# Sixteen modulation sums of the first mix moved from VectorE to GpSimd products with ScalarE sums

## The chip, the cores and the metric

One NeuronCore of a Trainium2 chip runs the whole program in one launch. The metric is the device time in microseconds (us). TensorE (PE) does the matrix products, VectorE (DVE) and ScalarE (ACT) the elementwise work, GpSimd (POOL) little, and the queue of SyncE (SP) issues nearly all the DMAs. Everything is float32; a weight tile is split into a high part (`ring_hi`) and a low part (`ring_lo`), and each product is made of three matmuls.

## The reference, cut to what matters

The first of two stacked networks has two layers. In each, a vector `c` gives 48 columns of modulation, which shift, scale and gate the mixer and the feed-forward part:

```python
c_act = jax.nn.silu(c)
for l in range(DEPTH):                       # DEPTH = 2
    mod = (c_act @ w_ada[l] + b_ada[l])[:, None, :]          # 6 * 1024 numbers
    shift1, scale1, gate1, shift2, scale2, gate2 = jnp.split(mod, 6, axis=-1)
    h = rms_norm(x, norm1_g[l]) * (1.0 + scale1) + shift1
    z = h @ w_in[l]                          # 14 column tiles of 128
    ...                                      # windowed attention, short convolution, pooling
    x = x + gate1 * (mix @ w_out[l])         # 8 column tiles
    h2 = rms_norm(x, norm2_g[l]) * (1.0 + scale2) + shift2
    x = x + gate2 * peer_ffn(h2, ...)
```

x has 256 tokens of 1024 features and lies with the features on the partitions. Modulation column k (of 48) is a dot product of `c_act` with 1024 weights for each of 128 partitions, so one column costs one 128x1024 weight unit (512 KB), one product with `CROW` (silu of c, the same row on all partitions) and one sum along the row.

## The kernel before

The program is a sequence of blocks; at the end of each all engines meet. The blocks that matter here are the mix of layer 0 and the mix of layer 1, which come from one loop over `layer` (the block that starts at L651), and the block behind each (L1175), which begins with a norm that needs modulation columns 24 to 39.

Weights come as units of 128x1024 into a ring of 8 slots (`stream`, L255: the load of unit n waits until unit n-7 has been used). ScalarE copies a unit to `ring_hi` (`split_high`, L351), VectorE subtracts it to `ring_lo` (`split_low`, L358, its instruction at L361), TensorE multiplies (24 matmuls for a unit, L309 to L311). The mix block has 14 input units; their results are drained by ScalarE (L866 to L871) and go into rotations (L983 to L987, VectorE), scores with their maxima (`take_score`, L994 and L996), exponentials on ScalarE (L884), probabilities (L1015), pooling (L1073 to L1080), convolution (L1085 to L1099) and the low parts of the mixed operand (`attended_low`, L1021). Then 8 output units follow; a first group of three units shares its passes (its last instruction is at L838), and VectorE adds each result, times the gate, to the residual (L1120, "x_mixed"). A norm over x ends the block: squares on ScalarE (L421), sums on TensorE (L427), the root (L435), its inverse on VectorE (L440).

Each engine's order is written out by hand. Each waits in that order, so whatever stands at the head of a queue holds back all behind it. In layer 0 alone 24 more modulation columns (`N_LATE`) are worked out inside the mix: the queue of SP loads their units into three buffers (`late_units`, L657, DMA at L662; the load of unit k waits for the sum of unit k-3), and VectorE does product and sum in one instruction (`modulation`, L967, instruction at L971, which is followed by the read of its accumulator). Their places in VectorE's order: 4 behind the split of unit 3, 2 behind the second rotation, 3 behind the second pair of scores (L1055), 3 ahead of the first "x_mixed" (L1114), and 12 between the "x_mixed" of the output units. SP's order is: late units 0 to 5, the rest of the input units, late 6 to 8, output units 0 to 3, late 9 to 11, output units 4 to 7, and then the first 8 units of the next block (`S_WQ`) with late units 12 to 23 between them. GpSimd does three memsets in this block (L678 to L680) and nothing else. In layer 1 there are no late units.

Of the kernel before, what the change touches and what calls it, by code (L numbers as in the profile page):

```python
# [33 lines left out]
D = 1024  # L34
# [118 lines left out]
def program(nc, wstream, consts, mixconst, crow, xT, memT, pos, vec2, s5b, s5c, wglu, wdt, out):  # L153
    ctx = ExitStack()
    with ctx:
# [45 lines left out]
        def S(name):  # L201

            if name not in named:
                named[name] = pools[0][len(named)]
            return named[name]
# [49 lines left out]
        def stream(sp, u0, u1):  # L255

            for n in range(u0, u1):
                sp.wait_ge(units_used, n - (SLOTS - 1))
                sp.dma_start(RING[:, n % SLOTS, :], wstream[STREAM[n]]).then_inc(loaded[n % SLOTS], 16)
# [91 lines left out]
        def split_high(act, u, fresh):  # L351

            arrived(act.eng, u)
            if not fresh:
                act.eng.wait_ge(units_used, u - HIGHS + 1)
            act.mark(act.eng.activation(RING_HI[:, u % HIGHS, :], RING[:, u % SLOTS, :], ACT.Copy), "high")  # L356
# [268 lines left out]
        for layer in range(DEPTH):  # L625
# [19 lines left out]
            PU, P2, P4, P8, P16 = (a(2, T + 16) for _ in range(5))  # L645
            PL = a(2, T)
            MIX, MIX_LO, MIX_HI = a.split(8, T)
            ADB = [late[:, i, :] for i in range(3)]
            N_LATE = N_ADB - HOISTED if layer == 0 else 0
            VALUES, POOLED, CONV_X, CONV_C, CONV_B = 5, 6, 8, 10, 12  # L650
            with nc.Block() as block:  # L651
                @block.sync
                def _(sp):
                    sp.dma_start(AR[:, D:2 * D], mixconst).then_inc(S("mix_consts"), 16)
                    sp.dma_start(PK[:, :], wstream[layer * PER_LAYER + U_PARAMS + 1][:, 0:512]).then_inc(S("pool_keys"), 16)

                    def late_units(k0, k1):  # L657

                        for k in range(k0, min(k1, N_LATE)):
                            if k >= 3:  # L660
                                sp.wait_ge(S("modulated"), k - 2)
                            sp.dma_start(ADB[k % 3], wstream[layer * PER_LAYER + U_ADB + k])\  # L662
                                .then_inc(S(f"late{k % 3}"), 16)

                    late_units(0, 6)
                    stream(sp, S_IN + SLOTS, S_OUT)
                    late_units(6, 9)
                    stream(sp, S_OUT, S_OUT + 4)
                    late_units(9, 12)
                    stream(sp, S_OUT + 4, S_OUT + 8)  # L670
                    for i in range(N_OUT):
                        stream(sp, S_WQ + i, S_WQ + i + 1)
                        late_units(12 + 3 * i // 2, 12 + 3 * (i + 1) // 2)

                @block.gpsimd
                def _(pool):

                    pool.memset(VP, 0.0).then_inc(S("cleared"), 1)  # L678
                    pool.memset(CU, 0.0).then_inc(S("cleared"), 1)
                    pool.memset(PU, 0.0).then_inc(S("cleared"), 1)  # L680

                @block.tensor
                def _(pe):
# [168 lines left out]
                def _(sc):  # L852
# [3 lines left out]
                    def next_high(i):  # L856

                        split_high(act, S_IN + i, False)

                    def drain(i):  # L860

                        sc.wait_ge(units_used, used(S_IN + i))
                        src = PS[:, 2 + i % 3, 0:T]
                        if i < VALUES:
                            gain = L_KG if i == 0 else L_QG
                            act.mark(sc.activation(QSQ[:, i, :], src, ACT.Square), "qk_squares")  # L866
                            act.mark(sc.activation(Z[:, i, :], src, ACT.Copy, scale=LV[:, gain:gain + 1]), "z_copied")
                        elif i in (POOLED, POOLED + 1):
                            act.mark(sc.activation(PU[:, i - POOLED, 8:8 + T], src, ACT.Copy), "z_copied")
                        else:  # L870
                            act.mark(sc.activation(Z[:, i, :], src, ACT.Copy), "z_copied")  # L871

                    def head_std(n, bank, o, name):

                        act.wait("head_sums", n)
                        act.mark(sc.activation(QS[:, o], PS[:, bank, o], ACT.Sqrt, bias=EPS_COL, scale=1.0 / 64), name)

                    def exponentials(j):

                        act.wait("maxes", 2 * j + 2)  # L880
                        o = slice(4 * j, 4 * j + 4)
                        act.mark(sc.activation(ESK[:, o], ESK[:, o], ACT.Exp), "sink_exp")
                        for i in range(4 * j, 4 * j + 4):
                            act.mark(sc.activation(SC[:, i, :], SC[:, i, :], ACT.Exp, bias=NMX[:, i:i + 1],  # L884
                                                   scale=QI[:, i:i + 1], accum_out=SUM[:, i:i + 1]), "exps")
# [7 lines left out]
                    def attended_high(j):  # L893

                        act.wait("attended", j + 1)
                        act.mark(sc.activation(MIX_HI[:, j, :], PS[:, j % 2, 0:T], ACT.Copy), "mix_high")

                    split_high(act, S_IN + PRE, True)
                    act.wait("cleared", 3)
                    drain(0)  # L900
# [3 lines left out]
                    drain(2)  # L904
                    head_std(1, 5, slice(16, 20), "key_std")
                    next_high(6)
                    drain(3)
                    next_high(7)
                    drain(4)
                    next_high(8)  # L910
                    head_std(5, 1, slice(0, 16), "q_std")
                    drain(5)
                    next_high(9)
                    drain(6)
                    next_high(10)
                    act.wait("v_turned", 1)
                    vt = PS[:, 5, 0:T].rearrange("p (k h d) -> p k h d", k=2, h=2)
                    act.mark(sc.activation(VP[:, :, 0, 0:64], vt[:, :, 0, :], ACT.Copy), "v_padded")
# [1 line left out]
                    drain(7)  # L920
                    exponentials(0)
                    next_high(11)
                    drain(8)
                    next_high(12)
                    exponentials(1)
                    drain(9)
                    next_high(13)
                    exponentials(2)
                    probs_copy(0)
                    probs_copy(1)  # L930
                    drain(10)
                    split_high(act, S_OUT, False)
                    exponentials(3)
                    act.mark(sc.activation(RT[:, 0:1], EPS_COL, ACT.Sqrt), "root_table")
                    attended_high(0)
# [1 line left out]
                    probs_copy(3)  # L937
                    drain(11)
                    split_high(act, S_OUT + 1, False)
                    attended_high(1)  # L940
                    probs_copy(4)
                    probs_copy(5)
                    split_high(act, S_OUT + 2, False)
                    attended_high(2)
                    probs_copy(6)
                    probs_copy(7)
# [6 lines left out]
                        act.mark(sc.activation(MIX_HI[:, 4 + i, :], MIX[:, 4 + i, :], ACT.Copy), "conv_high")  # L953
                    attended_high(3)
                    split_high(act, S_OUT + 3, False)
                    for i in range(N_OUT):
                        if i + HIGHS < N_OUT + PRE:
                            split_high(act, S_OUT + i + HIGHS, False)
                        square_chunk(act, i, "x_mixed")
# [4 lines left out]
                def _(dve):  # L964
# [87 lines left out]
                    take_score(2)  # L1052
                    take_score(3)
                    maxes(1)
                    modulation(6, 9)  # L1055
                    low(11)
                    take_score(4)
                    take_score(5)
# [52 lines left out]
                                                 ALU.subtract), "conv_low")  # L1111
                    attended_low(3)
                    split_low(v, S_OUT + 3, N_IN + 3 - PRE)
                    modulation(9, 12)  # L1114
                    if layer == 0:
                        v.wait("modulated", 8)
                        v(dve.tensor_tensor(MOD[:, 16:24], MOD[:, 16:24], LV[:, L_BADA + 16:L_BADA + 24], ALU.add), "mod")
                    for i in range(N_OUT):
                        dve.wait_ge(units_used, used(S_OUT + i))
                        v.mark(dve.scalar_tensor_tensor(X[:, i, :], PS[:, 2 + i % 3, 0:T], col(MOD[:, 16:24], i),  # L1120
                                                        X[:, i, :], ALU.mult, ALU.add), "x_mixed")
                        if i + HIGHS < N_OUT + PRE:
                            split_low(v, S_OUT + i + HIGHS, N_IN + i + HIGHS - PRE)
                        modulation(12 + 3 * i // 2, 12 + 3 * (i + 1) // 2)
                    if layer == 0:
                        v.wait("modulated", N_LATE)
                        v(dve.tensor_tensor(MOD[:, 24:40], MOD[:, 24:40], LV[:, L_BADA + 24:L_BADA + 40], ALU.add), "mod")
                        v(dve.tensor_scalar(S1G[:, 8:16], MOD[:, 32:40], 1.0, None, ALU.add), "mod")
                        v(dve.tensor_tensor(S1G[:, 8:16], S1G[:, 8:16], LV[:, L_N2:L_N2 + 8], ALU.mult), "mod")
# [1775 lines left out]
```

## Time and profile before

| | us |
|---|---|
| median of 3 runs | 2463.84 |
| lowest, highest | 2461.8, 2473.33 |
| the profiled execution | 2463.14 |
| its span, first to last instruction | 2461.3 |

| engine | busy us | share of the span | instructions |
|---|---|---|---|
| PE matmul | 2364.9 | 96% | 14280 |
| PE weight load | 2123.6 | 86% | 14280 |
| DVE | 1797.1 | 73% | 2913 |
| ACT | 1157.5 | 47% | 1707 |
| POOL | 148.3 | 6% | 141 |

Busy time is a share of the whole span; the two mix blocks are two short stretches of it, of about 115 and 100 us. In the timeline a row is: start, duration, engine, line, operation, output<-input, shape, count, and in brackets how long the engine sat idle before it and what ended the wait. Starts are us from the span's start. A row with a count above 1 merges instructions that follow each other without a gap. Consecutive VectorE instructions overlap a little in the records: a 128x1024 operation that shows 1.22 us is followed by the next one 1.13 to 1.15 us after its start.

### The profile page before, as it was taken

To read this page: it belongs to the slowest core of one execution; us is meant where nothing else is said; L and a number is where in the kernel's file an instruction comes from. 1 tells how busy PE (TensorE), PEld (TensorE's weight loads), DVE (VectorE), ACT (ScalarE), POOL (GpSimd) and SP (SyncE) were. 2 spreads that over 40 slices of the span, in tenths; PEclk is the share of its full clock that TensorE was granted. 3 is DMA by queue.
4 is the path that set the end of the run, shared out by engine and by line. 5 is a ranking of instruction groups with operands and counts; after the bars stand their busy time and mean duration, and the time that the engine had idled before them with its cause. 6 is when DMAs were issued, how large, how long until landed. Compare 5 with 4: busy or idle time off the path is not lost. (4 is left out here: it accounts for less than half of the span.)

```text
span 2461.3 us, 36638 instructions
## 1 busy us (share of the span) xinstructions
PE 2364.9 (96%) x14280; PEld 2123.6 (86%) x14280; DVE 1797.1 (73%) x2913; ACT 1157.5 (47%) x1707; POOL 148.3 (6%) x141
## 2 busy tenths in 40 slices
PE   4979999999999999999999999999999999999998
PEld 4879898888888888889899888888888888898998
DVE  7979997677667676678999676566767576555665
ACT  4542255444545454564135444455545523544554
POOL 0000153000000000000045100000000000000000
PEclk9989999999999999999999999999999999999999
DMA  9365544787676666434544586665555523343553
GB/s 356 134 227 163 157 124 149 267 298 240 233 242 231 239 231 223 148 111 139 177 135 125 188 299 220 204 216 187 189 188 191 191 78 108 124 148 126 189 186 107
DMA packets 133554, 460.63 MB, mean 187 GB/s; under 512 B 15152, under 2 KB 16432, under 8 KB 132912
## 3 DMA queue, kind: packets, MB, share of 16 engines
q1 hardware_dynamic: 133424, 458.90, 55.1%
q8 instruction: 82, 1.34, 0.2%
q14 instruction: 48, 0.39, 0.0%
HBM read 445.73 MB, written 13.11 MB: 186 GB/s over the span
## 5 line engine op out<-in xcount | busy, mean ns | idle before, releaser
L1654 DVE TENSOR_TENSOR ring_lo<-ring,ring_hi 128x1024 fp32r<-128x1024 f32 x421 | 506.9, 1222 | 88.6 <-ACT ring_hi L1557 88.6
L1557 ACT ACTIVATE ring_hi<-ring 128x1024 fp32r<-128x1024 f32 x421 | 435.0, 1054 | 134.0 <-PE banks L346 119.9
L319 PE MATMUL banks<-normed_lo,ring_hi 128*128 128x512 f32 x1344 | 477.9, 398 | 0.0
L344 PE MATMUL banks<-ring_hi,work_lo 128*128 128x512 f32 x1024 | 400.5, 391 | 8.0 <-DVE work_lo L1681 4.3
L345 PE MATMUL banks<-ring_lo,work_lo 128*128 128x512 f32 x1024 | 399.9, 391 | 0.0
L346 PE MATMUL banks<-ring_hi,work_lo 128*128 128x512 f32 x1024 | 399.1, 390 | 0.0
L320 PE MATMUL banks<-normed_lo,ring_lo 128*128 128x256 f32 x1344 | 377.2, 281 | 0.0
L319 PEld LDWEIGHTS banks<-normed_lo,ring_hi 128*128 128x128 f32 x1344 | 252.5, 188 | 61.8
L361 DVE TENSOR_TENSOR ring_lo<-ring,ring_hi 128x1024 fp32r<-128x1024 f32 x185 | 225.0, 1222 | 78.1 <-ACT ring_hi L356 77.5
L320 PEld LDWEIGHTS banks<-normed_lo,ring_lo 128*128 128x128 f32 x1344 | 253.8, 189 | 3.3
L1677 DVE TENSOR_TENSOR work<-banks,work 128x512 f32<-128x512 f32 x84 | 58.1, 692 | 249.2 <-ACT work L1563 249.2
L356 ACT ACTIVATE ring_hi<-ring 128x1024 fp32r<-128x1024 f32 x185 | 194.9, 1055 | 94.9 <-PE banks L311 53.5
L344 PEld LDWEIGHTS banks<-ring_hi,work_lo 128*128 128x128 f32 x1024 | 192.6, 188 | 50.8 <-DVE work_lo L1681 5.2
L346 PEld LDWEIGHTS banks<-ring_hi,work_lo 128*128 128x128 f32 x1024 | 192.6, 188 | 40.9
L1563 ACT ACTIVATE work<-banks 128x512 f32<-128x512 f32 x84 | 50.2, 597 | 372.4 <-PE banks L320 372.4
L345 PEld LDWEIGHTS banks<-ring_lo,work_lo 128*128 128x128 f32 x1024 | 192.6, 188 | 36.9
L309 PE MATMUL banks<-normed_lo,ring_hi 128*128 128x256 f32 x752 | 217.5, 289 | 1.2 <-DVE ring_lo L361 0.8
L310 PE MATMUL banks<-normed_lo,ring_hi 128*128 128x256 f32 x752 | 213.4, 284 | 0.0
L311 PE MATMUL banks<-normed_lo,ring_lo 128*128 128x256 f32 x752 | 213.3, 284 | 0.0
L1363 POOL TENSOR_TENSOR one_hots<-one_hots,routes 128x512 f32<-128x512 f32 x128 | 138.9, 1085 | 579.9 <-DVE one_hots L1426 573.0
L1240 PE MATMUL banks<-work,ring 128*128 128x256 f32 x736 | 159.5, 379 | 0.0
L1240 PEld LDWEIGHTS banks<-work,ring 128*128 128x128 f32 x736 | 139.5, 190 | 18.8
(387 smaller groups left out, 4357.4 us busy)
## 6 DMA issues: line engine op xcount, KB each, us to landing
ring<-wstream SPq DMA_DIRECT2D x716, 512.0 KB, 3.3
arena<-wstream SPq DMA_DIRECT2D x96, 512.0 KB, 5.7
spill<-one_hots SPq DMA_DIRECT2D x44, 256.0 KB, 4.2
rstd<-spill SPq DMA_DIRECT2D x16, 256.0 KB, 4.1
pool_and_keys<-spill SPq DMA_DIRECT2D x14, 256.0 KB, 4.1
routes<-spill SPq DMA_DIRECT2D x14, 256.0 KB, 4.8
residual<-xT SPq DMA_DIRECT2D x1, 1024.0 KB, 7.8
arena<-mixconst SPq DMA_DIRECT2D x2, 512.0 KB, 4.2
```

The source lines that it names most:

```text
L309: pe.matmul(dst, w_hi[:, o], hi[:, k, :], start=(k == 0), stop=False)
L310: pe.matmul(dst, w_hi[:, o], lo[:, k, :], start=False, stop=False)
L311: mm = pe.matmul(dst, w_lo[:, o], hi[:, k, :], start=False, stop=(k == KD - 1))
L319: pe.matmul(dst, w_hi[:, o], HR[:, k, :], start=(k == 0), stop=(k == KD - 1), skip_group_check=True)
L320: mm = pe.matmul(dst[:, 0:T], w_lo[:, o], HR[:, k, 0:T], start=False, stop=(k == KD - 1), skip_group_check=True)
L344: pe.matmul(dst, hi[:, t], w_hi[:, o], start=first, stop=False)
L345: pe.matmul(dst, hi[:, t], w_lo[:, o], start=False, stop=False)
L346: mm = pe.matmul(dst, lo[:, t], w_hi[:, o], start=False, stop=last)
L361: v.mark(v.eng.tensor_tensor(RING_LO[:, u % SLOTS, :], RING[:, u % SLOTS, :], RING_HI[:, u % HIGHS, :].bitcast(F32), ALU.subtract), "split")
L1240: mm = pe.matmul(dst, RING[:, u % SLOTS, o], H32[:, k, :], start=(k == 0), stop=(k == KD - 1))
L1557: sc.activation(RING_HI[:, u % HIGHS, :], RING[:, u % SLOTS, :], ACT.Copy)\
L1654: dve.tensor_tensor(RING_LO[:, u % SLOTS, :], RING[:, u % SLOTS, :], RING_HI[:, u % HIGHS, :].bitcast(F32), ALU.subtract).then_inc(S("spli ...
```

## The change

`N_LATE` becomes 8 (columns 16 to 23, which the gate of this mix needs). The other 16 columns (24 to 39) become "shared" units with three buffers of their own. For each: SP loads it, GpSimd multiplies it in place by `CROW`, and ScalarE copies it in place with an accumulated sum into its modulation column. Unit n's load waits for the sum of unit n-3. The three orders are written out anew. Layer 1 has none of it; only its SP order is written in another form.

```diff
+            shared = a(3, D)
-            N_LATE = N_ADB - HOISTED if layer == 0 else 0
+            N_LATE = KD if layer == 0 else 0
+            N_SHARED = 2 * KD if layer == 0 else 0
 ...
+                    def shared_units(n0, n1):
+                        for n in range(n0, min(n1, N_SHARED)):
+                            if n >= 3:
+                                sp.wait_ge(S("gathered"), n - 2)
+                            sp.dma_start(shared[:, n % 3, :], wstream[layer * PER_LAYER + U_ADB + KD + n])\
+                                .then_inc(S(f"shared{n % 3}"), 16)
-                    late_units(0, 6)
-                    stream(sp, S_IN + SLOTS, S_OUT)
-                    late_units(6, 9)
-                    stream(sp, S_OUT, S_OUT + 4)
-                    late_units(9, 12)
-                    stream(sp, S_OUT + 4, S_OUT + 8)
+                    late_units(0, 3)
+                    shared_units(0, 2)
+                    late_units(3, 6)
+                    shared_units(2, 4)
+                    for i in range(SLOTS, N_IN):
+                        stream(sp, S_IN + i, S_IN + i + 1)
+                        shared_units(i - 4, i - 3)
+                    late_units(6, KD)
                     for i in range(N_OUT):
-                        stream(sp, S_WQ + i, S_WQ + i + 1)
-                        late_units(12 + 3 * i // 2, 12 + 3 * (i + 1) // 2)
+                        shared_units(10 + i, 11 + i)
+                        stream(sp, S_OUT + i, S_OUT + i + 1)
+                    stream(sp, S_WQ, S_WQ + SLOTS)
 ...  # gpsimd, behind the three memsets
+                    for n in range(N_SHARED):
+                        pool.wait_ge(S(f"shared{n % 3}"), 16 * (n // 3 + 1))
+                        pool.tensor_tensor(shared[:, n % 3, :], shared[:, n % 3, :], CROW, ALU.mult)\
+                            .then_inc(S("shared_product"), 1)
 ...  # scalar
+                    def gather(n0, n1):
+                        for n in range(n0, min(n1, N_SHARED)):
+                            c = 16 + KD + n
+                            act.wait("shared_product", n + 1)
+                            act.mark(sc.activation(shared[:, n % 3, :], shared[:, n % 3, :], ACT.Copy,
+                                                   accum_out=MOD[:, c:c + 1]), "gathered")
 ...  # vector
-                    modulation(6, 9)
+                    modulation(6, KD)
-                    modulation(9, 12)
-                        modulation(12 + 3 * i // 2, 12 + 3 * (i + 1) // 2)
-                        v.wait("modulated", N_LATE)
+                        v.wait("gathered", N_SHARED)
```

The sums stand in ScalarE's order as follows: sum 0 behind the split of input unit 6; 1 and 2 behind 7; 3 behind 8; 4 and 5 behind 9; 6 behind 10; 7 behind 11; 8 behind 12; 9 behind 13; 10 behind output unit 0; 11 behind output unit 1; 12 and 13 behind output unit 2, ahead of the third `attended_high`; 14 and 15 behind output unit 3.

## Rows read from the trace of the kernel before

**Rows 1.** Windows: stretch, length, busy PE, PEld, DVE, ACT, POOL, PEclk, DMA share, GB/s
```profile
45.95:107.32 61.37, 55.90 (x402) 51.78 (x401) 58.08 (x111) 37.31 (x84) 0.00 (x0) 0.94 0.54 189
121.16:155.52 34.36, 22.68 (x162) 21.91 (x160) 26.34 (x43) 10.25 (x16) 0.00 (x0) 0.81 0.81 306
...
1022.00:1081.28 59.28, 55.43 (x405) 51.42 (x405) 48.02 (x93) 36.32 (x83) 0.00 (x0) 0.97 0.35 116
1094.63:1115.22 20.59, 19.38 (x162) 19.03 (x160) 12.11 (x16) 10.30 (x16) 0.00 (x0) 1.00 0.59 205
```

**Rows 2.** Timeline of VectorE, output units of layer 0, to the next block
```profile
121.16 0.48 DVE L1120 SCALAR_TENSOR_TENSOR residual<-banks,modulation,residual 128x256 f32<-128x256 f32 x1 [1.88 <-PE banks L838]
...
127.19 1.23 DVE L971 CUSTOM_DVE_ANT_0 arena<-arena 128x1024 f32<-128x1024 f32 x1 [3.72 <-DMA arena<-wstream]
...
152.85 0.18 DVE L1127 TENSOR_TENSOR modulation<-modulation,layer_vectors 128x16 f32<-128x16 f32 x1
...
155.52 0.87 DVE L452 SCALAR_TENSOR_TENSOR work<-residual,scale_gain,banks 128x256 f32<-128x256 f32 x2 [1.89 <-PEq L651]
```

**Rows 3.** Timeline of VectorE, output units of layer 1, to the next block
```profile
1094.63 0.48 DVE L1120 SCALAR_TENSOR_TENSOR residual<-banks,modulation,residual 128x256 f32<-128x256 f32 x1 [5.33 <-PE banks L838]
...
1113.69 0.17 DVE L440 RECIPROCAL token_rstd<-token_rstd 128x2 f32<-128x2 f32 x1 [1.55 <-ACT token_rstd L435]
1115.22 0.87 DVE L452 SCALAR_TENSOR_TENSOR work<-residual,scale_gain,banks 128x256 f32<-128x256 f32 x2 [1.37 <-PEq L651]
```

**Rows 4.** Groups of VectorE from 45.95 to 107.32: busy, mean ns | idle before
```profile
L361 DVE TENSOR_TENSOR ring_lo<-ring,ring_hi 128x1024 fp32r<-128x1024 f32 x13 | 15.8, 1219 | 0.5 <-ACT ring_hi L356 0.5
L971 DVE CUSTOM_DVE_ANT_0 arena<-arena 128x1024 f32<-128x1024 f32 x9 | 10.6, 1219 | 1.0 <-DMA arena<-wstream 1.0
L996 DVE TENSOR_REDUCE arena<-arena 128x2 f32<-128x512 f32 x8 | 5.5, 687 | 0.3
L994 DVE TENSOR_TENSOR arena<-banks,arena 128x512 f32<-128x512 f32 x8 | 5.4, 681 | 0.0
...
L985 DVE TENSOR_TENSOR arena<-banks,rope 128x256 f32<-128x256 f32 x5 | 2.1, 418 | 0.5 <-PE banks L705 0.5
...
L1021 DVE TENSOR_TENSOR part_at<-banks,part_at 128x256 fp32r<-128x256 f32 x3 | 1.3, 422 | 0.2 <-ACT part_at L896 0.2
...
L1039 DVE TENSOR_TENSOR arena<-arena,banks 128x256 f32<-128x256 f32 x1 | 0.4, 414 | 0.0
```

**Rows 5.** GpSimd's products in the feed-forward block of layer 0, and VectorE beside them
```profile
L1363 POOL TENSOR_TENSOR one_hots<-one_hots,routes x128: 1040/1042/1997, 292.7 to 1366.4; 128x512 f32<-128x512 f32 x128
...
296.51 1.95 POOL L1363 TENSOR_TENSOR one_hots<-one_hots,routes 128x512 f32<-128x512 f32 x1 [0.56 <-DVE one_hots L1426]
...
310.19 3.30 POOL L1363 TENSOR_TENSOR one_hots<-one_hots,routes 128x512 f32<-128x512 f32 x3 [2.29 <-DVE one_hots L1426]
...
296.35 1.22 DVE L1434 TENSOR_TENSOR ring_lo<-ring,work_lo 128x1024 fp32r<-128x1024 f32 x1
...
308.90 3.47 DVE L1426 TENSOR_TENSOR one_hots<-routes,banks 128x1024 f32<-128x1024 f32 x3
312.67 1.90 DVE L1434 TENSOR_TENSOR ring_lo<-ring,work_lo 128x1024 fp32r<-128x1024 f32 x1 [0.30 <-ACT work_lo L1335]
```

**Rows 6.** Groups of ScalarE from 45.95 to 121: busy, mean ns | idle before
```profile
L356 ACT ACTIVATE ring_hi<-ring 128x1024 fp32r<-128x1024 f32 x14 | 14.8, 1057 | 2.3 <-PE banks L311 2.3
...
L884 ACT ACTIVATION_READ_ACCUMULATOR arena<-arena 128x1 f32 x16 | 3.0, 188 | 0.0
```

**Rows 7.** DMA issues from 36 to 160: count, KB, median us to landing
```profile
arena<-wstream SPq DMA_DIRECT2D x24, 512.0 KB, 5.7
ring<-wstream SPq DMA_DIRECT2D x22, 512.0 KB, 5.4
```

**Rows 8.** Windows of a starved stretch of layer 0, columns as in rows 1
```profile
80.00:88.00 8.00, 3.85 (x16) 2.74 (x16) 7.76 (x16) 6.14 (x20) 0.00 (x0) 0.78 0.71 264
88.00:93.00 5.00, 5.00 (x30) 4.95 (x29) 4.76 (x12) 1.20 (x3) 0.00 (x0) 0.66 0.00 1
```

More of the change, by code:

```diff
@@ L906, in _ @@
                     next_high(6)
+                    gather(0, 1)
                     drain(3)
                     next_high(7)
+                    gather(1, 3)
                     drain(4)
                     next_high(8)
+                    gather(3, 4)
                     head_std(5, 1, slice(0, 16), "q_std")
@@ L913, in _ @@
                     next_high(9)
+                    gather(4, 6)
                     drain(6)
                     next_high(10)
+                    gather(6, 7)
                     act.wait("v_turned", 1)
@@ L922, in _ @@
                     next_high(11)
+                    gather(7, 8)
                     drain(8)
                     next_high(12)
+                    gather(8, 9)
                     exponentials(1)
@@ L927, in _ @@
                     next_high(13)
+                    gather(9, 10)
                     exponentials(2)
@@ L932, in _ @@
                     split_high(act, S_OUT, False)
+                    gather(10, 11)
                     exponentials(3)
@@ L939, in _ @@
                     split_high(act, S_OUT + 1, False)
+                    gather(11, 12)
                     attended_high(1)
@@ L943, in _ @@
                     split_high(act, S_OUT + 2, False)
+                    gather(12, 14)
                     attended_high(2)
@@ L955, in _ @@
                     split_high(act, S_OUT + 3, False)
+                    gather(14, 16)
                     for i in range(N_OUT):
```

## The prediction, made before the changed kernel was run

> **What bounds the kernel now.** The page of the profile says that PE is 96% busy over the span, which tells little of one block of 115 us. I went from the page to the timeline of the layer 0 mix, engine by engine, and then to the same block in layer 1, because layer 1 runs the same code without the 24 late modulations: it is a measured picture of what is left when they are gone. The mix falls into two parts with different limits.
>
> The front, from the split of input unit 3 to the third low part of the attention, lasts 61.37 us, and VectorE is busy for 58.08 of them [rows 1]. It is the bound there, idle only for about 1.7 us, while PE waits for it in places. Layer 1 does the same stretch in 59.28 us with 48.02 us of VectorE [rows 1], so the nine modulations of layer 0 in the front cost only 2.1 us in all, since layer 1's VectorE idles where they stood.
>
> The back, from the first "x_mixed" to the first norm instruction of the next block, is another matter. It takes 155.52 - 121.16 = 34.36 us in layer 0 [rows 2] and 1115.22 - 1094.63 = 20.59 us in layer 1 [rows 3]. VectorE carries 12 modulations there, waits up to 3.72 us at a time for their units [rows 2], and DMA moves 306 GB/s at a busy share of 0.81 against 205 at 0.59 [rows 1]. PE works 22.68 us in the one and 19.38 in the other [rows 1]; it ran at a mean granted clock of 0.81 in layer 0, and the clock fell behind its waits.
>
> **The change, part by part.**
>
> *Back.* All 12 modulations and the loads for them leave; what remains is layer 1's back. The gain is 34.36 - 20.59 = 13.8 us. The three small modulation operations at the end stay (layer 1 lacks them). They fit into the 1.55 us for which layer 1's VectorE waits for the root [rows 3], as they are three operations of the size of L1127, 0.18 us [rows 2]; without that cover they would cost 0.6. VectorE's new wait for "gathered" 16 stands in front of them, and behind it the inverse of the norm, for which the end of the block waits. Load 15 goes out once sum 12 is done, that is near 108, and needs 5.7 us to land [rows 7]; the product and the sum take 3 us more. That is over long before 140, while PE does its output units. I count nothing for it.
>
> *Three modulations ahead of the first "x_mixed" (L1114).* VectorE waits 1.88 us for PE behind them [rows 2]; they were hidden, and removing them gives nothing.
>
> *Front, VectorE removed.* `modulation(6, 9)` loses one of three: 1.15 us of a VectorE that is the bound.
>
> *Front, ScalarE added.* Sums 0 to 13 lie ahead of the third attended low part. A 128x1024 copy is 1.06 us, the read of an accumulator 0.19 [rows 6] and partly covered, so a sum is 1.1 to 1.25 us and fourteen are 15 to 17.5. ScalarE is busy for 37.3 of the 61.4 us [rows 1], so there is room, and it is late at few places. I take 0 for it, with 2 as the other end: sums 12 and 13 stand directly ahead of the attended high part for which VectorE waited 0.2 us [rows 4].
>
> *Front, SP.* Each load of a shared unit waits for a sum, and behind it in the queue stand the ring's loads. Input unit 8 now goes out behind shared unit 3, that is after sum 0. That is some 6 us later than now and still ahead of its split on VectorE by more than the 5.4 us of a landing [rows 7]. Late 6 and 7 stand behind shared 9 (sum 6), and have the scores between. I count 0 and watch it.
>
> *Front, GpSimd added.* Fourteen products of 128x1024, for which there is no row. The nearest is 128x512 at 1.042 us [rows 5]; twice that is 2.08 us. The question is what they do to VectorE, and here rows speak. VectorE's subtraction at 312.67 reads two tensors of SBUF and took 1.90 us in place of 1.22. GpSimd's last product of that group ended at 310.19 + 3.30 = 313.49, and 312.67 + (1.90 - 1.22) = 313.35: the subtraction stood still until GpSimd was done, less 0.14 us [rows 5]. The other way round, GpSimd's product at 296.51 took 1.95 in place of 1.04 because a subtraction had begun at 296.35, ending at 297.57 [rows 5]. The three operations from 308.90, with one input in SBUF and one in PSUM, ran beside GpSimd at the usual length [rows 5]. So a product excludes every VectorE operation with two SBUF inputs for its own time less 0.14: 2.08 - 0.14 = 1.94 us.
>
> The Trainium skill says this as a rule (SBUF — State Buffer, section "SBUF: two separate sides"): the pair of ports that VectorE and GpSimd share is "an exclusive lock, not a bandwidth split", held for a whole instruction, also against a VectorE operation with two SBUF inputs. By that rule, the trace agrees. The skill's GPSIMD Engine Reference (section "Elementwise — side-by-side cycle accounting") gives 4497 ns for 2048 elements, hence an estimate of 2.25 us for 1024; with it the fourteen would be 2.4 us dearer in all.
>
> How much of the front excludes GpSimd? Free of it are the operations that read a bank: L994 (5.4), L985 (2.1), two of L1021 (0.8) and L1039 (0.4), and I count L996 (5.5), with one input, among them: 14.2 us [rows 4]. Of the 61.37, less 1.7 idle, that leaves 45.5 us, less the 1.15 that goes: 44.3. Fourteen holds are 27.2 us. If every free microsecond ran under a product, the front would need 44.3 + 27.2 = 71.5 us, or 10.2 more than now. If none did, 44.3 + 27.2 + 14.2 = 85.7, and with the old idle time 87.4: 24.4 to 26 more. Both ends hold whichever engine gets the pair first, for no order lets the two overlap.
>
> I take a value by walking the products through VectorE's order, each as soon as its unit has landed and the running operation is over. Products 0 and 1 fall among modulations and hide nothing. Products 2 to 9 fall among splits, rotations and modulations, where a free piece is 0.4 us long. The long free pieces are the four pairs of scores, 2.6 us each; ahead of two of them no product is due, since sum 7 waits behind the first exponentials, and the later ones cover about 1 us each of products 10 and 11. All told about 4 us of the 14.2 are used: 24.4 - 4 = 20.4, a front of about 82 us. Both parts of the front's end are nearly the same in the layers, and products 14 and 15 fall into the 9 us in which PE works alone on the first output group.
>
> *Sum.* The profiled execution is 2463.14 us, 0.7 below the median of the runs. + 20.4 (front) - 13.8 (back) = + 6.6, so 2469.7 us.
>
> **The rivals.**
>
> *A. The products hide in the free pieces.* If VectorE wins each time that both ask, a product waits until VectorE does something free, and starts with it: nearly all of the score pairs are used. The front then grows by 10.2 to 14, and the kernel moves by -3.6 to +0.2: 2459.5 to 2463.3, say 2461.5. For it: in the rows a product that found VectorE running got its turn in front of a free operation [rows 5]; no row shows two excluding operations in sequence with a product waiting. Against it: the sums stand in fixed places on ScalarE, and a product that comes late holds back splits. Chance 0.19.
>
> *B. Faster: the products stand in nobody's way.* This needs VectorE's 45 us of excluding work not to be excluded here, for instance because another row form decides it than the one in rows 5. The front would lose 1.15 us and the back 13.8: 2448.2. Rows 5 speak plainly against it. Chance 0.13.
>
> *C. Slower by more: PE falls to its lower clock in a starved front.* VectorE's delays make PE wait before each unit. In the stretch from 80 to 88 PE was busy for 3.85 of 8 us, and in the next 5 us the granted clock was 0.66, between the two levels of 1.2 and 2.4 GHz [rows 8]. The 30 matmuls of those 5 us took 0.167 us each [rows 8], against 55.90 / 402 = 0.139 over the front [rows 1]: 0.7 us more on a unit of 24. If that comes on all eleven units of the front and lies in the chain unit, drain, score, VectorE each time, it adds 8 us. It decides from the point at which PE's waits repeat before most units and VectorE then waits for PE in turn. With it and with little of the free time used: 20.4 + 8 - 13.8 = + 14.6, 2477.7. Chance 0.18.
>
> *D. The change doesn't do what it says in the back:* sums or loads come so late that the back keeps waiting. The SP queue could do it, if shared 13 to 15 held back output units. Five us of the 13.8 would be lost with the front as forecast: 2474.7. Chance 0.05.
>
> **How the numbers follow.** The forecast has 0.45, from 2464 to 2475. With A (0.19), C (0.18) and D (0.05) the range goes from 2459.5 to 2480; B (0.13) is left out below. A measurement of this kernel can tell about 0.5%, or 12.3 us, from no change: below 2451.5 is faster, above 2476.2 slower. Faster is B, 0.13. Slower is most of C and the upper tail of the forecast, 0.17. The rest, 0.70, is within 0.5%.
>
> **What would show it.** In the changed kernel's trace: VectorE's splits (L361's group) and modulations in the front with a mean of well over 1.22 us, many near 3, and none so long in layer 1; GpSimd's products at 2.1 us where they meet nothing and up to 3.2 where they meet a split; the front, from the split of input unit 3 to the third attended low part, near 82 us; the back near 20.6 us. The forecast is wrong if the splits stay at 1.22 us, if the products are much shorter than 2.08, or if the front's length follows ScalarE's sums (VectorE idle before L361 waiting for L356) rather than long VectorE operations.

## The result, and the profile after

The changed kernel takes 2472.05 us (median of 20 runs) against 2463.81 us for the kernel before (20 runs): a ratio of 1.0036, 95% interval 1.0029 to 1.0042. It is 8.2 us slower; the forecast was 2469.7.

| | before | after |
|---|---|---|
| span of the profiled execution | 2461.3 | 2469.4 |
| DVE busy us, instructions | 1797.1, 2913 | 1805.2, 2881 |
| ACT busy us | 1157.5 | 1173.0 |
| POOL busy us | 148.3 | 192.6 |
| front: split of input unit 3 to the third attended low part | 61.37 | 83.55 |
| between: to the first x_mixed | 13.84 | 14.39 |
| back: to the first norm instruction of the next block | 34.36 | 20.67 |

VectorE lost 16 modulations of 1.15 us and is nevertheless busy 8 us longer. These are the three stretches of the table, in the columns of [rows 1]; the first and the last of them answer to its first two rows:

```profile
45.86:129.41 83.55, 65.93 (x414) 59.81 (x414) 81.71 (x108) 51.85 (x112) 41.89 (x15) 0.88 0.55 199
129.41:143.80 14.39, 13.01 (x100) 12.24 (x100) 8.70 (x14) 5.74 (x13) 2.56 (x1) 1.00 0.40 140
143.80:164.47 20.67, 19.38 (x162) 18.97 (x160) 12.49 (x19) 10.24 (x16) 0.00 (x0) 0.99 0.59 205
```

The back is layer 1's: 20.67 against 20.59 us, and both DMA figures are the same [rows 1]. The front lost ground: VectorE is busy 81.7 of 83.6 us with 108 instructions, where it was 58.1 with 111 [rows 1]. The timeline of VectorE at the start of the front shows how:

```profile
48.15 1.22 DVE L1008 CUSTOM_DVE_ANT_0 arena<-arena 128x1024 f32<-128x1024 f32 x1
49.29 0.08 DVE L1008 DVE_READ_ACCUMULATOR2_ANT modulation<- 128x1 f32 x1
49.29 3.40 DVE L1008 CUSTOM_DVE_ANT_0 arena<-arena 128x1024 f32<-128x1024 f32 x1
52.63 0.08 DVE L1008 DVE_READ_ACCUMULATOR2_ANT modulation<- 128x1 f32 x1
52.63 3.40 DVE L1008 CUSTOM_DVE_ANT_0 arena<-arena 128x1024 f32<-128x1024 f32 x1
```

And GpSimd from its first product on:

```profile
48.96 5.99 POOL L696 TENSOR_TENSOR arena<-arena 128x1024 f32<-128x1024 f32 x2 [8.96 <-DMA arena<-wstream]
...
83.60 2.93 POOL L696 TENSOR_TENSOR arena<-arena 128x1024 f32<-128x1024 f32 x1 [1.20 <-DMA arena<-wstream]
86.87 2.39 POOL L696 TENSOR_TENSOR arena<-arena 128x1024 f32<-128x1024 f32 x1 [0.34 <-DMA arena<-wstream]
97.74 2.36 POOL L696 TENSOR_TENSOR arena<-arena 128x1024 f32<-128x1024 f32 x1 [8.49 <-DMA arena<-wstream]
```

The first product found a modulation running, waited for it, and then went ahead of the next modulation, which therefore took 3.40 us in place of 1.22; the second product did the same. (A row of GpSimd with a count of 2 or 3 merges products, and its duration includes such waits; a product that meets nothing takes 2.36 us.) Even small operations pay the whole price when they come behind a product's start. Rows of the changed kernel:

```profile
64.57 2.23 DVE L1069 COPY arena<-arena 128x256 f32<-128x256 f32 x1
...
80.13 2.55 DVE L1024 TENSOR_TENSOR arena<-arena 128x256 f32<-128x256 f32 x1
...
84.23 0.68 DVE L1031 TENSOR_TENSOR arena<-banks,arena 128x512 f32<-128x512 f32 x1
84.95 0.69 DVE L1033 TENSOR_REDUCE arena<-arena 128x2 f32<-128x512 f32 x1
85.55 0.68 DVE L1031 TENSOR_TENSOR arena<-banks,arena 128x512 f32<-128x512 f32 x1
86.26 0.69 DVE L1033 TENSOR_REDUCE arena<-arena 128x2 f32<-128x512 f32 x1
86.99 2.29 DVE L1040 TENSOR_TENSOR arena<-arena 128x4 f32<-128x4 f32 x1
...
100.67 2.20 DVE L1042 TENSOR_SCALAR arena<-arena 128x4 f32<-128x4 f32 x1
...
125.70 2.46 DVE L1128 TENSOR_SCALAR arena<-arena,layer_vectors 128x256 f32<-128x256 f32 x1
```

The same lines of code in the kernel before (a copy, the rotation's last step, the 128x4 operations, the convolution step):

```profile
58.05 0.29 DVE L1032 COPY arena<-arena 128x256 f32<-128x256 f32 x1
...
67.33 0.43 DVE L987 TENSOR_TENSOR arena<-arena 128x256 f32<-128x256 f32 x1
...
72.06 0.16 DVE L1003 TENSOR_TENSOR arena<-arena 128x4 f32<-128x4 f32 x1
...
72.46 0.17 DVE L1005 TENSOR_SCALAR arena<-arena 128x4 f32<-128x4 f32 x1
...
105.72 0.35 DVE L1091 TENSOR_SCALAR arena<-arena,layer_vectors 128x256 f32<-128x256 f32 x1
```

The score pair from 84.23 to 86.99 ran at its normal length beside the product of 83.60; the product of 86.87 came when only 0.1 us of the pair was left and held off L1040 behind it. Of the 15 products in the front, 12 lengthened one VectorE operation each: three modulations and a split by 2.16 to 2.18, one first and two last steps of rotations, a copy, two of the 128x4 operations, a pooling sum and a convolution step by 1.7 to 2.2. Together that is 24.9 us, 2.08 on the mean. Three products (those of 83.60, 97.74 and 104.67) hid under score pairs. The front's account closes: 61.37 + 24.9 - 1.15 (one modulation less) - 1.45 (idle of 1.67 became 0.22) = 83.7, measured 83.55.

Two SBUF inputs are not the whole condition. Three of the twelve long operations have a single tensor of SBUF as input: the copy (2.23 us where it took 0.29 before), L1042, and L1128, which multiplies it by one number per partition. `TENSOR_REDUCE`, which has a single input too, kept its 0.69 us beside a product.

### The profile page after: what moved, and what is told of

Same layout as the page of the kernel before. It is cut to its first block and busy times, and to the rows that moved or that the text cites. A ratio compares the mean times of both kernels' runs of the same rounds, so it can differ in the third digit from the quotient of the medians.

```text
span 2469.4 us, 36654 instructions
## 1 busy us (share of the span) xinstructions
PE 2370.8 (96%) x14280; PEld 2126.8 (86%) x14280; DVE 1805.2 (73%) x2881; ACT 1173.0 (48%) x1739; POOL 192.6 (8%) x157
## 5 line engine op out<-in xcount | busy, mean ns | idle before, releaser
L1712 DVE TENSOR_TENSOR work<-banks,work 128x512 f32<-128x512 f32 x84 | 58.1, 692 | 249.4 <-ACT work L1598 249.4
```

## The experiments

Theory L says that the products hold off VectorE. Its rival, theory S, says that the front's time comes from what was added around them: ScalarE's sums and the new order of the load queue. Times are medians; a ratio is against the kernel before, timed on the same chip, whose median was 2464 to 2465 us there.

### Products of 8 columns (e1_tiny)

```diff
-pool.tensor_tensor(shared[:, n % 3, :], shared[:, n % 3, :], CROW, ALU.mult)
+pool.tensor_tensor(shared[:, n % 3, 0:8], shared[:, n % 3, 0:8], CROW[:, 0:8], ALU.mult)
```

> The changed kernel, but each GpSimd product covers 8 of its 1024 columns; the other 1016 columns are summed without the factor. Loads, waits and ScalarE sums are the same. Theory L (the products hold off VectorE; in the profile of the changed kernel 12 of the 15 front products each lengthen one VectorE operation by about 2.1 us, 24.9 us in all): the front falls from 83.6 us to about 60, VectorE has no operation lengthened by more than 0.2 us, and the time is 2472 - 24 = 2448. Theory S (ScalarE's sums and the new order of the load queue cost the front its time): the front stays above 80 us and the time at 2470.

2455.7 us, ratio 0.9965 (0.995 to 0.9979), thus 16 us less than the changed kernel. No VectorE operation of the front was lengthened by more than 0.15 us, as L says, but the front was 68.3 us and not 60. VectorE's timeline has three long waits there:

```profile
52.68 1.23 DVE L1008 CUSTOM_DVE_ANT_0 arena<-arena 128x1024 f32<-128x1024 f32 x1 [2.04 <-DMA arena<-wstream]
...
81.21 1.22 DVE L1008 CUSTOM_DVE_ANT_0 arena<-arena 128x1024 f32<-128x1024 f32 x1 [2.91 <-DMA arena<-wstream]
...
114.29 0.42 DVE L1058 TENSOR_TENSOR part_at<-banks,part_at 128x256 fp32r<-128x256 f32 x1 [4.03 <-ACT part_at L913]
```

The first two are late units 3 and 6, which now load behind shared units; in the kernel before the first of these waits was 0.98 and the second 0. The third is the attended high part behind sums 12 and 13; the two sums take 2.1 us directly ahead of it, and ScalarE had waited 2.3 us for TensorE ahead of its split before them. Relative to the kernel before the three are 1.1 + 2.9 + 3.8 = 7.8 us, which is the gap to the expectation. In the changed kernel the same three waits are 0, 0 and 0.22: the held-off VectorE covers them. So L holds for the bulk, and S is not nothing: its 7.8 us lie under L's.

### Product and sum on VectorE, the rest as changed (e2_vector)

```diff
-                    for n in range(N_SHARED):            # gpsimd: the products
-                    gather(...)                          # scalar: the sums
 ...
+    # vector, behind the split of the same unit as each of ScalarE's sums:
+    dve.wait_ge(S(f"shared{n % 3}"), 16 * (n // 3 + 1))
+    v.mark(dve.tensor_tensor_reduce(shared[:, n % 3, :], shared[:, n % 3, :], CROW, 1.0, 0.0,
+                                    ALU.mult, ALU.add, MOD[:, c:c + 1]), "gathered")
```

> The changed kernel with the same 16 shared units, buffers and loads, but product and sum are made by one VectorE instruction, behind the same splits; GpSimd and ScalarE have no part in it. Fourteen of them, 1.15 us each, come to lie on VectorE in the front. Theory L: 24.9 us of held-off time goes, 16.1 us come, so the front is about 75 us and the time 2472 - 8.8 = 2463, the time of the kernel before. Theory S: without ScalarE's 14 sums, but with the new load order and 16.1 us more VectorE work, it would stay near the changed kernel, 2466 to 2472.

2466.5 us, ratio 1.0013 (1.0003 to 1.0022): 5.5 us faster than the changed kernel, not 8.8, and inside S's range too, so the time alone does not decide between them. The trace does. No operation is long; the front is 77.81 us: 61.37 - 1.15 + 12 sums of 1.15 = 74.0, and 3.8 us more, nearly all of it idle time. Its two waits for DMA, 1.72 and 1.78 us, were 0.98 and 0 in the kernel before; they are the load order's. Two sums I had put in the front lie behind it. What the run shows is the exchange rate: in this front a modulation made wholly by VectorE costs it 1.15 us, and one that is taken off it costs it 2.1 where its product holds something off, or 24.9 / 15 = 1.7 on the mean with the three that hid.

### Products of 512 columns (e3_half)

```diff
+pool.tensor_tensor(shared[:, n % 3, 0:512], shared[:, n % 3, 0:512], CROW[:, 0:512], ALU.mult)
```

> The changed kernel, but each product covers 512 of its 1024 columns; the rest is summed without the factor. A product is then 1.04 us and holds VectorE off for about 0.9. Theory L: about 12 operations lengthened by 0.9 us, 11 us in all in place of 24.9, time 2472 - 14 = 2458. If the cost were a fixed one for each product (dispatch, semaphores), it would stay near 2470. Theory S: 2470.

2459.83 us, ratio 0.9987 (0.9977 to 0.9997). Twelve operations are lengthened, by 0.62 to 1.10 us, 11.0 us in all, where 1024 columns gave twelve and 24.9. The front is 70.65 us, and its account closes too: 61.37 + 11.0 - 1.15 - 0.6 (idle of 1.67 became 1.04) = 70.6. A product that met nothing, and a split that met one:

```profile
78.00 1.27 POOL L696 TENSOR_TENSOR arena<-arena 128x512 f32<-128x512 f32 x1 [1.11 <-DMA arena<-wstream]
```

```profile
70.05 2.29 DVE L361 TENSOR_TENSOR ring_lo<-ring,ring_hi 128x1024 fp32r<-128x1024 f32 x1
```

The price goes with the size of the product, so it is neither dispatch nor semaphores. A product of this form that meets nothing takes 1.26 to 1.28 us, not the 1.04 of the row I had scaled from.

### A memset in place of the product (e4_memset)

```diff
+pool.memset(shared[:, n % 3, :], 0.0)
```

> The changed kernel with a GpSimd memset of the 1024 columns (about 1.0 us, it writes and reads nothing) in place of the product; the sums are then of zeros. Theory L in the form that only a GpSimd operation which reads holds off a VectorE operation with two SBUF inputs: those keep 1.22 us, only VectorE's copy and one-tensor operations may be lengthened, and the time is that of the kernel with 8 columns, 2448. In the form that any GpSimd operation does it: up to 12 operations lengthened by 0.9 us, 2458.

2455.07 us, ratio 0.9968 (0.9954 to 0.9982), the time of the 8-column kernel as expected, though not the 2448 that I had for both: the same three waits as in e1_tiny stand here, 2.25, 2.19 and 3.31 us. GpSimd and VectorE at the first two memsets:

```profile
49.55 0.96 POOL L696 MEMSET arena<- 128x1024 f32 x1 [9.29 <-DMA arena<-wstream]
50.79 0.95 POOL L696 MEMSET arena<- 128x1024 f32 x1 [0.28 <-DMA arena<-wstream]
```

```profile
49.54 1.22 DVE L1008 CUSTOM_DVE_ANT_0 arena<-arena 128x1024 f32<-128x1024 f32 x1
...
108.08 1.05 DVE L1128 TENSOR_SCALAR arena<-arena,layer_vectors 128x256 f32<-128x256 f32 x1
```

The modulation beside the memset has its normal length, though both its inputs are in SBUF. The operation with one tensor of SBUF, L1128, took 1.05 us in place of 0.35: GpSimd's memset, which only writes, holds off that kind. Delays of this kind came up in two places of the front, 1.1 us in all; the other was L1042.

### An operation with one input in place of the product (e5_scalar)

```diff
+pool.tensor_scalar(shared[:, n % 3, :], shared[:, n % 3, :], 1.5, None, ALU.mult)
```

> The changed kernel with a GpSimd operation of one SBUF input (times a constant, in place, 128x1024) for the product; the sums are of other values. Theory L, with reading as the condition: VectorE operations with two SBUF inputs are held off for its whole length, be that 1 or 2 us, as they were not by the memset; at 1.0 us the time is about 2459, at 2.1 us 2471. If two inputs on both sides are needed for the hold, it is 2455, as with the memset.

2457.25 us, ratio 0.9973 (0.9962 to 0.9984). Both of my forms were off: the operation lasts 2.76 us or more, longer than the product, yet holds VectorE for less. GpSimd first, then VectorE:

```profile
58.69 2.85 POOL L696 TENSOR_SCALAR arena<-arena 128x1024 f32<-128x1024 f32 x1 [1.39 <-DMA arena<-wstream]
```

```profile
58.83 1.26 DVE L1020 TENSOR_TENSOR arena<-arena,rope 128x256 f32<-128x256 f32 x1
...
60.45 0.42 DVE L1024 TENSOR_TENSOR arena<-arena 128x256 f32<-128x256 f32 x1
...
61.00 0.68 DVE L1069 COPY arena<-arena 128x256 f32<-128x256 f32 x1
```

L1020 with two SBUF inputs waited until 58.83 + 0.84 = 59.67, one us after GpSimd's start; L1024, of the same kind, ran freely at 60.45, while GpSimd's operation lasted until 61.54. The copy at 61.00 was held off once more. Twelve operations of the front were delayed, 9.4 us in all: ten with two inputs by 0.76 to 0.85 each, this copy by 0.39 and L1128 by 0.78. The front of 71.1 us is 61.37 + 9.4 - 1.15 + 1.5 of additional idle time. It looks as if GpSimd reads in the first microsecond and writes later, but the trace does not show its two sides apart, so that reading is an inference.

### Six buffers, all 24 modulations on VectorE (v1_six)

```diff
-            late = a(3, D)
+            late = a(6, D)            # load k waits for sum k-6
 ...
-  # modulations: 4 + 2 + 3 in the front, 3 ahead of x_mixed, 12 among the output units
+  # modulations: 4, 1, 1, 1, 3 in the front (behind low(3), low(4), turn(1), low(7), maxes(1)),
+  # 6 ahead of x_mixed, 8 one by one behind each x_mixed
```

> The kernel before, all 24 modulations still single instructions on VectorE, but with six buffers and new places: 10 in the front (there layer 1's VectorE stands idle for four of the gaps), 6 while TensorE works alone on the first output group, 8 one by one behind the x_mixed. GpSimd and ScalarE have no part. If the 13.8 us of the back came from loads that were late and modulations that stood together, the back falls to about 21 us, the front stays at 61.4, the stretch between grows by 1.6: 2464 - 12 = 2452. If the back needs fewer modulations to get shorter, it stays above 27 us and the time at 2457 or more.

2454.98 us, ratio 0.9963 (0.9952 to 0.9974). Front 62.81, between 15.43, back 23.04: the back gave 11.3 us and not 13, and the front 1.4 more than planned. So most of the gain of the changed kernel's back, 11.3 of 13.7 us, needs neither GpSimd nor ScalarE. The run has earlier loads, modulations that are spread out, and 8 of them in the back in place of 12; it does not show what each of the three is worth.

### The same with four products under score pairs (v2_timed), and those four untimed (v3_untimed)

```diff
+  # order of the units: 6 VectorE, 2 GpSimd, 2 VectorE, 2 GpSimd, 12 VectorE; buffer p % 6
+                    for n, split in enumerate((9, 10, 11, 12) if layer == 0 else ()):
+                        pool.wait_ge(*landed(p))         # p: place of product n in the order above
+                        pool.wait_ge(S("split"), split - PRE + 1)      # v3_untimed: left out
+                        pool.tensor_tensor(ADB[p % 6], ADB[p % 6], CROW, ALU.mult).then_inc(S("shared_product"), 1)
 ...
+  # ScalarE's sums behind next_high(10), next_high(12) and, two, behind probs_copy(1)
+  # VectorE: 4, 1, 1, 2 in the front, 5 ahead of x_mixed, 7 among the output units
```

> As v1_six, but four of the modulations are GpSimd products with ScalarE sums, each product made to wait until VectorE has made the split ahead of a pair of scores, so that it starts with 2.8 us of VectorE work that reads a bank or a single tensor; 8 on VectorE in the front, 5 in the group's shade, 7 behind the x_mixed. Theory L: a product of 2.36 us fits into the 2.8 us and holds nothing off, no VectorE operation is lengthened by more than 0.3 us; front about 60, back 20.9, time 2449. If a product costs VectorE its time wherever it stands, the front is 68 and the time 2457.

> v2_timed without that wait: the same four products start as soon as their unit has landed. Theory L: three or four of them meet VectorE operations with two SBUF inputs, each lengthened by about 2.1 us; front 6 to 8 us longer than in v2_timed, time 2455 to 2457. If the place does not matter, the same as v2_timed.

v2_timed: 2450.51 us, ratio 0.9949 (0.9933 to 0.9965), faster than both kernels and 4.5 us faster than v1_six; the slowest run of v2_timed, 2452.19, is ahead of the fastest of v1_six, 2452.5. v3_untimed: 2458.18 us, ratio 0.9977 (0.9966 to 0.9987). They differ in one wait on GpSimd. The fronts are 59.88 and 67.07 us. In v2_timed, GpSimd and VectorE at the first pair:

```profile
69.35 2.42 POOL L716 TENSOR_TENSOR arena<-arena 128x1024 f32<-128x1024 f32 x1 [29.10 <-DVE ring_lo L361]
```

```profile
69.22 0.69 DVE L1043 TENSOR_TENSOR arena<-banks,arena 128x512 f32<-128x512 f32 x1
69.95 0.69 DVE L1045 TENSOR_REDUCE arena<-arena 128x2 f32<-128x512 f32 x1
70.55 0.68 DVE L1043 TENSOR_TENSOR arena<-banks,arena 128x512 f32<-128x512 f32 x1
71.26 0.69 DVE L1045 TENSOR_REDUCE arena<-arena 128x2 f32<-128x512 f32 x1
71.98 0.16 DVE L1052 TENSOR_TENSOR arena<-arena 128x4 f32<-128x4 f32 x1
```

The product ends at 71.77, just ahead of L1052, which has its 0.16 us again; in the changed kernel the same line of code took 2.29. None of VectorE's operations is lengthened. In v3_untimed all four products met one, 7.9 us in all (GpSimd, then VectorE):

```profile
53.36 2.50 POOL L715 TENSOR_TENSOR arena<-arena 128x1024 f32<-128x1024 f32 x1 [13.30 <-DMA arena<-wstream]
57.52 2.40 POOL L715 TENSOR_TENSOR arena<-arena 128x1024 f32<-128x1024 f32 x1 [1.66 <-DMA arena<-wstream]
```

```profile
53.54 3.40 DVE L1019 CUSTOM_DVE_ANT_0 arena<-arena 128x1024 f32<-128x1024 f32 x1
...
57.65 2.54 DVE L1035 TENSOR_TENSOR arena<-arena 128x256 f32<-128x256 f32 x1
```

The difference in time, 7.7 us, and that of the fronts, 7.2, agree with what was held off.

### The covered costs undone, with full and with tiny products (e6_repaired, e7_tiny_repaired)

```diff
-                    late_units(6, KD)                    # behind shared 9
+                    # late 6 behind input unit 10, late 7 behind input unit 11
 ...
-                    gather(12, 14)                       # ahead of attended_high(2)
-                    gather(14, 16)
+                    gather(12, 15)                       # behind output unit 3
+                    # sum 15 among the output units, its load behind output unit 7
```

> The changed kernel with its full products, but late units 6 and 7 load behind input units 10 and 11, and ScalarE makes sums 12 and 13 behind output unit 3 and no longer ahead of the third attended high part, sum 15 among the output units. In the profile with tiny products VectorE waited 2.9 us for late unit 6 and 4.0 us for ScalarE at these two places; in the changed kernel itself it waited 0.2 in all. If the long VectorE operations cover these two costs, undoing them gains 0 to 1 us: 2471 to 2472. If the costs add to the held-off time, it gains about 7: 2465.

> The same two edits on the kernel with products of 8 columns. Nothing covers the waits here: both go, front 68.3 - 2.9 - 3.8 = 61.6, time 2455.7 - 6.7 = 2449. If the waits come back elsewhere (ScalarE's sums pushed to another critical place), it stays above 2453.

With full products: 2471.65 us, ratio 1.0028 (1.0018 to 1.0038), against 1.0036 (1.0029 to 1.0042) for the changed kernel, not to be told from it. Its front has no idle time left and thirteen lengthened operations, 26.2 us. With tiny ones: 2451.34 us, ratio 0.9947 (0.9929 to 0.9965), 4.4 us less than e1_tiny; in the traces the three stretches together are 4.3 us shorter. The wait for late unit 6 is gone; VectorE still waits 2.13 us for late unit 3 and 2.04 for the third attended high part, half of what it was:

```profile
52.79 1.23 DVE L1010 CUSTOM_DVE_ANT_0 arena<-arena 128x1024 f32<-128x1024 f32 x1 [2.13 <-DMA arena<-wstream]
...
108.68 0.42 DVE L1060 TENSOR_TENSOR part_at<-banks,part_at 128x256 fp32r<-128x256 f32 x1 [2.04 <-ACT part_at L914]
```

So the expectation of 2449 was missed by the part of ScalarE's wait that did not come from the two sums. The pair nevertheless shows what it was made for: the same edit is worth 4.4 us without the products and nothing measurable with them.

## Why the prediction was right

**The direction and the mechanism held.** The forecast was 2469.7 us, + 6.6 on the profiled execution; the span grew by 8.1 and the median by 8.2. The two terms of the sum, and a third stretch that I had left at 0:

- *The back*, forecast as layer 1's 20.59 us, came out at 20.67: 13.7 us gained. Reading the same code in the layer without the modulations was worth more than any sum of instructions. VectorE's new wait for the last sum cost nothing, and the three small operations fitted in the wait for the root, as said.
- *The front*, forecast at 20.4 us more, came out at 22.2. Four sizes inside it were off and partly cancelled. The product is 2.36 us alone, not 2 x 1.042 = 2.08; the row I had scaled from was of another operand form, and no run shows whether that is the reason. The estimate of 2.25 from the figure of the Trainium skill (GPSIMD Engine Reference, section "Elementwise — side-by-side cycle accounting") was nearer than the row. The time held off per product was 2.08 and not 1.94. There were 15 products in the front, not 14: the fifteenth did not wait for PE's lone stretch. Against that, three products hid whole under score pairs, 3 x 2.08 = 6.2 us, where I had counted about 4, and they were others than the ones that I had walked there. With the right number of products my other sizes give 15 x 1.94 less 4 = 25.1, close to the 24.9 found: dearer products and more hiding cancelled, which is luck.
- *The stretch between* grew by 0.5 us; I had it at 0. The last product held off a convolution step by 2 us there.

The three stretches together grew by 9.0 us and the span by 8.1, so the rest of the program was 0.9 us shorter in this execution.

**The condition was too narrow.** The prediction let a product exclude VectorE operations with two SBUF inputs. Three of the twelve, 6.1 of the 24.9 us, have one. The sum did not suffer, because it took every operation as excluding that it had not named as free, and of the one-input operations only `TENSOR_REDUCE` was named. And a hold does not always last as long as GpSimd's instruction: in e5_scalar VectorE's L1020 went on after 1.0 us of GpSimd's 2.85.

**The steps costed at nothing.** SP's order and ScalarE's sums were given 0, with 2 us as ScalarE's other end. They cost nothing in the changed kernel, but only under the cover of the held-off VectorE: e1_tiny, where the cover is gone, shows 4.0 us for the loads and 3.8 for ScalarE's lateness, 2.1 of them its two sums. I named the cover for the small operations at the end and not for these two, and my reason for SP (units still land in time) was wrong for late units 3 and 6.

**Rival A** (the products wait for free pieces) is refuted by the modulations at 49.29 and 52.63: of VectorE operations in close sequence with a product waiting, the product goes first. **Rival B** (no exclusion) is refuted by the 12 long operations; e1_tiny and e7_tiny_repaired show what it would have been worth: 2451 to 2456 us and not the 2448 that I worked out, because of the same covered costs. **Rival C** (PE at its lower clock) is seen but did not decide: the granted clock of the front fell from 0.94 [rows 1] to 0.88, yet VectorE, idle for 0.2 us of it, never waited for PE. **Rival D** did not come: the back is layer 1's.

## What to carry to other kernels

Work taken off VectorE and given to GpSimd is not free for VectorE: here a 1.15 us operation was replaced by a GpSimd product that stopped VectorE for about 2.1 us wherever it met an operation with two SBUF inputs, a copy, or a tensor_scalar. It costs nothing if it starts with a stretch of VectorE work that it does not hold off (here operations that read a bank, and `TENSOR_REDUCE`) and that lasts longer than it does; one wait that fixes the start was worth 7.7 us for four products. Before moving work between engines, look where its time really comes from: six buffers and a better spread on the same engine, with no work moved, gave a kernel 17 us faster than the move, and putting four well timed products in place of four of its modulations made it 4.5 us faster still.

## What the runs showed of the hardware that was not expected

- A waiting GpSimd product goes ahead of the next VectorE operation even when VectorE's operations follow each other without a gap (product begun at 48.96, modulation of 49.29 lengthened from 1.22 to 3.40 us).
- A GpSimd product of two SBUF tensors holds off VectorE operations with one SBUF tensor too: a copy 128x256 (0.29 to 2.23 us) and tensor_scalars (0.17 to 2.20, 0.35 to 2.46). It did not hold off `TENSOR_REDUCE` 128x512 (0.69 us beside it) nor operations that read a bank.
- A GpSimd product 128x512 took 1.04 us with one form of its operands [rows 5] and 1.26 with another (e3_half); 1024 columns took 2.36.
- A GpSimd operation with one input and a constant took 2.76 us for 128x1024, more than the product of two tensors, but held off VectorE operations with two inputs for only 0.76 to 0.85 us (e5_scalar).
- A GpSimd memset of 0.95 us did not delay a VectorE operation with two SBUF inputs, but lengthened one with a single SBUF tensor by 0.7 us (e4_memset).
